# An earlier gain product in the post-norm, earlier transposes, splits between eviction halves, and one unused 160-byte tile

## The reference

```python
def _rmsnorm(t, g):
    t32 = t.astype(jnp.float32)
    t32 = t32 * lax.rsqrt(jnp.mean(t32 * t32, axis=-1, keepdims=True) + RMS_EPS)
    return t32.astype(t.dtype) * g
...
        f = _swiglu(_rmsnorm(h, ffn1_pre_g[l]), ffn1_w_gate[l], ffn1_w_up[l], ffn1_w_down[l])
        h = h + 0.5 * _rmsnorm(f, ffn1_post_g[l])
...
        h = h + _rmsnorm(merged @ w_out[l], mix_post_g[l])
```

## Time and profile before

| | |
|---|---|
| median of 3 runs | 1970.82 us (1969.3 to 1971.09) |
| the profiled execution's own time | 1963.71 us |
| its span | 1961.9 us |
| TensorE busy (matmuls) | 1880.7 us, 96% |
| VectorE, ScalarE busy | 1204.2 us, 61%; 1032.3 us, 53% |
| mean granted TensorE clock | 0.989 |
| read from HBM | 330.97 MB, 169 GB/s |

### The profile page before, as it was taken

The page is one execution under the profiler, slowest core; times in us unless marked ns, Lnnn a source line. Parts: engine busy times, 40 slices in busy tenths (PEclk is TensorE's granted clock), DMA queues, the critical chain, the costliest instruction groups (busy, mean ns, idle before and its releaser), DMA issues.

```text
span 1961.9 us, 27084 instructions
## 1 busy us (share of the span) xinstructions
PE 1880.7 (96%) x10521; PEld 1638.5 (84%) x10521; DVE 1204.2 (61%) x1828; ACT 1032.3 (53%) x1671; POOL 101.0 (5%) x78
## 2 busy tenths in 40 slices
PE   7999999999999999999999999999989998889998
PEld 6888899987788878888998778887989986769996
DVE  5555656676655465536666665546757746656763
ACT  6545545545644464436455564446466646355652
POOL 0000001110000000000111000000002200001210
PEclk9999999999999999999999999999989999999999
DMA  7755574455565556656544456555646655336652
GB/s 247 212 188 173 164 198 138 138 163 166 180 197 185 186 168 197 187 161 167 153 141 150 164 173 206 190 182 160 192 137 179 187 190 147 104 88 173 183 188 103
DMA packets 357887, 333.83 MB, mean 170 GB/s; under 512 B 25338, under 2 KB 303488, under 8 KB 357760
## 3 DMA queue, kind: packets, MB, share of 16 engines
q1 hardware_dynamic: 357760, 332.11, 55.3%
HBM read 330.97 MB, written 1.05 MB: 169 GB/s over the span
## 4 chain that ended last, share of the span: by engine, by line
PE 84%; DVE 9%; ACT 4%; issue 1%; DMA 1%; SPq 0%; DVEq 0%; ACTq 0%
PE bank L1572 19%; PE bank L1574 19%; PE bank L1573 19%; PE bank L1583 7%; PE bank L1584 7%; PE bank L1585 7%; DVE wlo L994 4%; PE bank L1589 2%; ACT whi L535 1%; ACT uhi L561 1%; DVE ulo L1031 1%; DMA raw<-in_w_in 1%; ACT fx_s L721 1%; DVE fx_s L1223 1%; DVE bank L1023 0%
## 5 line engine op out<-in xcount | busy, mean ns | idle before, releaser
L994 DVE TENSOR_TENSOR wlo<-raw,whi 128x1024 fp32r<-128x1024 f32 (+3 forms) x638 | 750.0, 1183 | 494.2 <-ACT whi L535 491.6
L535 ACT ACTIVATE whi<-raw 128x1024 fp32r<-128x1024 f32 (+3 forms) x638 | 646.9, 1024 | 503.2 <-PE bank L1574 405.0
L1572 PE MATMUL bank<-whi,uhi 128*128 128x512 f32 (+2 forms) x1200 | 461.1, 384 | 23.7 <-DVE gates L1168 11.1
L1574 PE MATMUL bank<-wlo,uhi 128*128 128x512 f32 (+2 forms) x1200 | 449.2, 374 | 0.0
L1573 PE MATMUL bank<-whi,ulo 128*128 128x512 f32 (+2 forms) x1200 | 448.8, 374 | 0.0
L1583 PE MATMUL bank<-uhi,whi 128*128 128x256 f32 x1088 | 313.5, 288 | 1.7 <-DVE ulo L1031 1.7
L1584 PE MATMUL bank<-ulo,whi 128*128 128x256 f32 x1088 | 309.9, 285 | 0.0
L1585 PE MATMUL bank<-uhi,wlo 128*128 128x256 f32 x1088 | 309.7, 285 | 0.0
L1572 PEld LDWEIGHTS bank<-whi,uhi 128*128 128x128 f32 x1200 | 227.0, 189 | 60.4 <-issue 17.4
L1574 PEld LDWEIGHTS bank<-wlo,uhi 128*128 128x128 f32 x1200 | 226.7, 189 | 34.2
L1573 PEld LDWEIGHTS bank<-whi,ulo 128*128 128x128 f32 x1200 | 227.3, 189 | 31.7
(11 more groups left out here) (279 smaller groups left out, 1736.8 us busy)
## 6 DMA issues: line engine op xcount, KB each, us to landing
raw<-in_ffn_w_up SPq DMA_DIRECT2D x352, 256.0 KB, 3.4
raw<-in_ffn_w_down SPq DMA_DIRECT2D x264, 256.0 KB, 2.9
raw<-in_ffn_w_gate SPq DMA_DIRECT2D x176, 256.0 KB, 2.9
raw<-in_w_gate SPq DMA_DIRECT2D x128, 192.0 KB, 2.7
raw<-in_w_in SPq DMA_DIRECT2D x80, 256.0 KB, 3.9
raw<-in_a_w_in SPq DMA_DIRECT2D x48, 256.0 KB, 3.3
raw<-in_w_mem_kv SPq DMA_DIRECT2D x32, 256.0 KB, 3.3
raw<-in_w_out SPq DMA_DIRECT2D x32, 256.0 KB, 2.8
```

What stands on the lines that cost most here:

```text
L535: act.activation(whi[n % SLOTS][:, 0:w], raw[n % RAW][:, 0:w], ACT.Copy).then_inc(hi_ready, 1)
L994: dve.tensor_tensor(wlo[n % SLOTS][:, 0:w], raw[n % RAW][:, 0:w], whi[n % SLOTS][:, 0:w].bitcast(F32), ALU.subtract).then_inc(lo_ready, 1)
L1572: pe.matmul(dst, xh, wh, start=start, stop=False)
L1574: return pe.matmul(dst, xh, wl, start=False, stop=stop)
```

## The change

It has four parts. The post-norm multiplies each half by the gain in place, half 0 before the wait for the root and half 1 behind the first addition, and a fused operation then scales by the reciprocal and adds. `tail` issues its transposes behind the second and third chunk of tile 1 instead of the third and fourth, and the second layer's mixer issues tile 1's behind its third and fourth chunk instead of the third and fifth. In `between` one split moves between the two eviction halves of tile 0, and the splits of n0+4 and n0+5 and the squares of tile 0 move behind tile 1's evictions. A tile `line` of 128 x 40 floats is declared behind `lst` and used by nothing.

```diff
         lst = sb("lst", [P, 12])
+        sb("line", [P, 40])
...
             def between(b, n0):   # ScalarE
 
                 post_root(b, 0)
+                split_to(n0 + 2)
+                u_high(b, 0, 0)
                 split_to(n0 + 3)
-                u_high(b, 0, 0)
                 u_high(b, 0, 1)
                 post_root(b, 1)
-                split_to(n0 + 5)
-                h_squares(b, 0)
                 u_high(b, 1, 0)
                 u_high(b, 1, 1)
-                h_squares(b, 1)
-                h_root(b, 0)
-                h_root(b, 1)
+                split_to(n0 + 5)
+                for t in range(TT):
+                    h_squares(b, t)
+                for t in range(TT):
+                    h_root(b, t)
...
             def post_norm(b, t):   # VectorE
+                f = [bank[acc(b) + 2 * t + nb][:, :] for nb in range(2)]
+
+                def times_gain(nb):
+                    dve.wait_ge(sq_f, 4 * i + 2 * t + nb + 1)
+                    dve.tensor_tensor(f[nb], f[nb], gpost[:, half[nb]], ALU.mult).then_inc(scaled, 1)
+
+                def add(nb):
+                    dve.wait_ge(scaled, 4 * i + 2 * t + nb + 1)
+                    h = H[:, t, half[nb]]
+                    dve.scalar_tensor_tensor(h, f[nb], stat(b, t, PREC), h, ALU.mult, ALU.add).then_inc(h_ready, 1)
+
                 dve.wait_ge(sq_f, 4 * i + 2 * t + 1)
                 dve.tensor_scalar(stat(b, t, PB), stat(b, t, SS), s / DM, s * EPS, ALU.mult, ALU.add).then_inc(pbias, 1)
+                dve.wait_ge(gp_loaded, 16 * (i + 1))
+                times_gain(0)
                 dve.wait_ge(proot, 2 * i + t + 1)
                 dve.reciprocal(stat(b, t, PREC), stat(b, t, PROOT)).then_inc(prec, 1)
-                dve.wait_ge(gp_loaded, 16 * (i + 1))
                 dve.wait_ge(prec, 2 * i + t + 1)
-                for nb in range(2):
-                    f = bank[acc(b) + 2 * t + nb][:, :]
-                    dve.scalar_tensor_tensor(f, f, stat(b, t, PREC), gpost[:, half[nb]], ALU.mult, ALU.mult).then_inc(scaled, 1)
-                residual(b, t, lambda nb: dve.wait_ge(scaled, 4 * i + 2 * t + nb + 1))
+                add(0)
+                times_gain(1)
+                add(1)
...
                 post_norm(b, 0)        # between, VectorE
                 split_to(n0 + 2)
                 u_low(b, 0, 0)
+                split_to(n0 + 3)
                 u_low(b, 0, 1)
-                split_to(n0 + 3)
                 post_norm(b, 1)
-                split_to(n0 + 5)
-                h_bias(b, 0)
                 u_low(b, 1, 0)
                 u_low(b, 1, 1)
-                h_bias(b, 1)
-                h_rstd(b, 0)
-                h_rstd(b, 1)
+                split_to(n0 + 5)
+                for t in range(TT):
+                    h_bias(b, t)
+                for t in range(TT):
+                    h_rstd(b, t)
...
                     ins.then_inc(w_used, 1)        # tail, TensorE
-                    if j >= n - 2:
-                        turns(j - n + 2)
+                    if n - 3 <= j < n - 1:
+                        turns(j - n + 3)
...
-                        if l and t == 0 and i in (2, 4):        # mixer, TensorE
-                            stream_turn(b, 1, i // 2 - 1)
+                        if l and t == 0 and i in (2, 3):
+                            stream_turn(b, 1, i - 2)
```

## The result

The changed kernel took 1951.51 us (median of 4 runs, 1946.5 to 1953.85); the kernel before took 1970.06 beside it. The ratio is 0.9905, 95% interval [0.9888, 0.9922]: 18.6 us less.

What follows compares the result with a forecast made beforehand. The chain of waits put 84% of the span on TensorE and 9% on VectorE. Savings of 12.4 + 0 + 0 + 3.3 + 13.1 = 28.8 us took the median from 1970.8 to 1942 us, range 1936 to 1960.

Steps and rivals of the forecast that it cites:

- the padding is inert: Rival: the 6.7 ns come from something else, such as the tile's place in a partition; 1955 us, chance 0.22.
- the forecast alone: Whole kernel, reordering and padding both paying as summed: 1942 us, span 1937 to 1948, chance 0.60.
- Post-norm, transposes and splits at b = 2, 3, 5, 6: Four junctions between norms: tile 1's first matmul starts 3.1 us sooner at each, 12.4 us in all.
- the merges: Two mixers: earlier transposes move `merged_turn`, and the 1.8 us wait shrinks; 1.1 us saved each, 2.2 in all.
- The step by step sum for b = 3: At b = 3: transposes find tile 1 ready, first matmul at about 702.35 instead of 705.76; 3.1 us taken.
- b = 4: Second mixer: first wait shrinks, but TensorE stands about 3.5 us before chunk n0+4; 0, bounds -3 to +3.
- b = 1: The 0.60 us wait goes, but splits reach TensorE about 0.8 us late; 0, bounds -0.8 to +1.5.
- b = 8, 7, 9: Transposes one chunk earlier: -0.7 us at b = 8, where ScalarE's eviction waits; -0.2 each at 7 and 9.
- the reordering: All junctions and mixers, the change without its padding: 15.7 us saved.
- The unused tile: Padding puts stage tiles on a multiple of 128 bytes, shortening 2184 matmuls by 6.0 ns: 13.1 us, bounds 0 to 14.6.
- The slower rival: Chunks n0+4 and n0+5 split late stop TensorE at six junctions and its clock falls; 1988 us, chance 0.05.

Runs made afterwards that it cites:

- no_line: The changed kernel without the unused tile `line`: 1953.87 us, ratio 0.9922.
- before_again: The kernel before, unchanged, run once more for another profile: 1964.37 us.
- pad_32: The changed kernel with the unused tile cut from 160 to 32 bytes: 1943.38 us, ratio 0.9866.
- u_low: The changed kernel without `line`, tiles reordered: `uhi`, `ulo` at byte 16512, stage tiles between 32896 and 126656, `raw`, `whi`, `wlo` above: 1931.35 us, ratio 0.981.
- early_split: pad_32 with the next two chunks' split put ahead of tile 1's `uhi` and `ulo` at b = 1 and 4: 1938.08 us, ratio 0.9836.
- gain_only: The kernel before with the new post-norm alone, transposes and splits as before: 1967.36 us, ratio 0.9984.
- tail_only: The kernel before with the tail's transposes one chunk earlier and nothing else: 1957.03 us, ratio 0.9948.
- u_high: The changed kernel without `line`, tiles reordered: `uhi`, `ulo` moved up to byte 175808, `hhi`, `ohi`, `lhi` down to 82048: 1945.38 us, ratio 0.9876.

## Why the prediction was right, and where it was not

The measured 1951.5 lies in the range, 9.5 us above the forecast and 3.5 under the rival "the padding is inert", 1955. It lies outside the 1937 to 1948 that the forecast alone allowed: the range holds it only because it was drawn out to that rival, and that rival is what happened.

*Post-norm, transposes and splits at b = 2, 3, 5, 6* (12.4 and 2.2 for the merges, 14.6): right. The stages show 4.55 + 3.12 + 4.53 + 3.22 = 15.4. The step by step sum for b = 3 said that the transposes find tile 1 ready, that the first `ulo` wait goes too, and that 3.1 us are gained; the trace has no wait there and 3.12 (3.31 at the junction itself). That the splits behind tile 1 have enough cover held: no `wlo` wait at any of the four.

*Which part gives it*: this I had summed as one. The runs show that the parts do not add. The medians (3.3 and 10.6 alone, 16 together) can't show it, their intervals are too wide, but the stages do: at b = 3 0.45 and 0.59 alone, 1.89 together, and 1.4 more with the new order of the splits.

*b = 4* (0, -3 to +3): the wait for `wlo` was put at about 3.5 us and is 3.18. The 0 came out by luck. Against the first profile, from which the sum was made, the stage is 2.6 us earlier in the changed kernel, whose clock fell (+0.6 was forecast for that), and 4.3 in no_line, whose clock held (-2.2 forecast). Of both, 3.07 is the slow stretch that the first execution happened to have; against before_again the changed kernel is 0.4 later and no_line 1.2 earlier. The sum took the old slow stretch from one window of 5 us (894 to 899) and put the same behind the new wait. The old one was 6.8 us long, and the new one 3.4 or absent. The Trainium skill (TensorE: Matmul & The Clock Gate, "Part 1: The HAM clock gate") says that the timing of the monitor that gates the clock is not tied to the kernel, so that equal code can ramp differently from run to run; 0.50 in one execution and 1.00 in the other behind waits of 3.01 and 2.99 us agree.

*b = 1* (0): -0.1, with a 0.73 us wait for `wlo` in place of the 0.60 for `H`. *b = 8, 7, 9* (-0.7, -0.2, -0.2): -1.07, -0.36, -0.30.

So the reordering was forecast at 15.7. The medians give 18.6 with the inert tile and, by the ratio, 15.4 without it (no_line). By stages it is 19.4 up to the latent attention, but 3.1 of that at b = 4 and 1.1 behind b = 7 are longer slow stretches of the first execution, which leaves 15.2. The forecast was right within what these runs can tell.

*The unused tile* (13.1): this step failed. It gave 0: `hhi` kept 0.2333 us, and no_line without the tile takes the same time. The observation was sound: 6.7 ns more for stationary tiles at another place, 2184 matmuls, and pad_32 gives back some 12 us by stages. What failed is "the rows differ in nothing else that I can find but the height of the address", together with the choice of 128 bytes as the unit. I compared each tile with a multiple of 128. `whi` and `uhi` are at 128 modulo 256, and the padding puts `hhi` at 0: both multiples of 128, half a period apart. The rival had its price right and its reason wrong: place matters, and 160 bytes is the wrong place. The Trainium skill (SBUF — State Buffer, the table under "Specifications (TRN2)") knows lines of 16 bytes only; all these starts are multiples of 16, and by that alone no order of tiles would change the time. The 0.2265 us of pad_32 against 0.2333 contradict it as a full account, while its verdict on this padding, no change, came true.

*The slower rival* (late splits stop TensorE at every border): the stall showed at b = 4, with 3.18 us, and with 0.73 at b = 1, and nowhere else.

## What to carry to other kernels

Where the same instruction with the same shape has two speeds in one kernel, compare the starts of both its SBUF operands with each other, not each with a round number, and try one moved by 32 or 64 bytes: here 32 bytes in place of 160 gave 8 us of 1951. It has to be measured by shape, since what was fastest at 512 columns was slowest at 256. When VectorE, ScalarE and TensorE hand a tile round, speeding up one of them moves the wait to the next; take the order on all three together, and then look for the one border where the next stage wants its data sooner than elsewhere. Before a split is moved off one engine's path, look what the other engine has queued ahead of the next hand-over: at b = 7 and 9 that made the move cost 1.1 us each. And read the granted clock beside every saving at a wait: at b = 4 it was 3.07 us between two executions of one kernel.

## What the runs showed of the hardware that I had not expected

- At 512 columns, a matmul with its weight load starts every 226.7 ns if the two tiles' starts agree modulo 256, and every 229.2 or 233.3 if not. At 256 columns the order turns: 120.0 with equal phases, 118.3 at 32 apart, 113.3 to 117.8 at 64. At 320 columns `vhi` was 146.7 at every phase tried. One stretch of each, u_low and then pad_32, (1460.9 - 1448.9)/102 = 0.1176 and (1460.8 - 1449.0)/99 = 0.1192 us (from the single starts 0.1176 and 0.1200):

```profile
L1596 PE MATMUL bank<-uhi,whi x35: 281/281/282, 1448.9 to 1460.9; 128*128 128x256 f32 x35
```

```profile
L1596 PE MATMUL bank<-uhi,whi x34: 283/283/283, 1449.0 to 1460.8; 128*128 128x256 f32 x34
```

- The phases do not fix the spacing alone. In u_low the same 256-column loop over the same tiles has a second, quicker spacing in other stretches, as here, (1389.5 - 1371.5)/159 = 0.1132 us; in the kernels with equal phases there is none:

```profile
L1597 PE MATMUL bank<-ulo,whi x54: 276/276/277, 1371.5 to 1389.5; 128*128 128x256 f32 x54
```

- The fastest median, u_low's 1931.35, stays unexplained. Its profiled execution took 1942.05, like pad_32, and the spacings give about the same: 2.5 ns more on 4728 matmuls and 2.5 less on 3600. Its three other runs took 1923.61 to 1933.83 at the same clock of 0.986 to 0.987. What was quicker in them no trace shows. One candidate: in the profiled one b = 7 and 9 had the slower of two spacings in both loops. With the quicker ones, 2063 matmuls by 4.4 ns and 528 by 4.3, it would have taken 11 us less (an estimate), 1931; it is not shown that the others had them. u_low's order together with early_split was not run.
- The short slow stretches in the mixers come and go. Whether kernels with faster matmuls have more of them (pad_32's clocks are 0.984 and 0.985, the changed kernel's 0.984 to 0.989) is open. All but one of the other kernels lose 5 to 7 us in the latent attention against the kernel before, gain_only and tail_only too, so it is no single part of the change. The one that does not, u_high (0.5 us), is also the only one of them without a third stretch at 0.50 there, 10.2 us long (1675.4 in the changed kernel). So the loss goes with that stretch; why it comes so regularly is open.
